# The chunked RWKV-7 recurrence of an encoder kernel: inverse and state in one unrolled body, 32x32 blocks transposed by VectorE, MLP down-products in a pair

## The chip, the cores and the metric

One core of a Trainium2 chip runs the kernel in one launch. The metric is device microseconds. Three runs of the kernel before took 2734.05, 2734.75 and 2739.23 us.

## The reference, cut to what matters

Two layers on a sequence of 1024 rows of 1024 columns. Layer 0 mixes with a gated convolution (512 columns) and RWKV-7 (8 heads of 64), layer 1 with windowed attention; each is followed by an MLP. All is float32. The change is in the RWKV-7 scan and in both MLPs:

```python
    def step(state, inp):
        r_t, w_t, k_t, v_t, a_t, b_t = inp
        sa = jnp.einsum("bhvk,bhk->bhv", state, a_t)
        state = (state * w_t[:, :, None, :] + sa[..., None] * b_t[:, :, None, :]
                 + v_t[..., None] * k_t[:, :, None, :])
        return state, jnp.einsum("bhvk,bhk->bhv", state, r_t)
...
def squared_relu_mlp(h, w_up, w_down):
    return jnp.square(jax.nn.relu(h @ w_up)) @ w_down
```

## The kernel before, in words

The residual, its norm and all weights of the running product lie in SBUF with model columns on the 128 partitions. Dense products are done in three passes of fp32r halves (`product`, L245): high times high, low times high, high times low. Stages follow each other: input projection, recurrence, output projection, MLP 0, QKV, attention, output, MLP 1.

**The recurrence** goes over NT = 8 chunks of 128 rows. For each chunk there are four pieces of work.
- prep (L634 to L768) makes a, b, k and r with their decays from the projected rows: lora products on TensorE (L665, L671), adds, a scan, and products on VectorE, sigmoids, exponentials and a root on ScalarE, squares summed and spread per head (L620, L626), the bonus (L686).
- the solve needs the inverse of a unit triangular 128x128 matrix for each of 8 heads. `chunk_pe` (L888) transposes a, b, k, v to token-major (L895), forms the masked products p1 and p2 (L913; VectorE masks them into mt_rb and nt_rk, L1050), starts the inverse tri_inv_t from pairs of rows (GpSimd L1106, L1109), transposes it (L923), and doubles the solved block in LEVELS = 6 levels. In levels 0 to 3 each is y = x_level times tri_inv (L947), copied by ScalarE (L1025), and then two products dt and dtt (L958, L961), which VectorE adds to the inverse and to its transpose (L1083, L1085); all are 128x128 per head, with masks x_level from GpSimd (L1113). Levels 4 and 5 work on 32x32 and 64x64 blocks (L847, L859, L862; L872, L884).
- the state part: w_t (L971), z (L975), u (L986), the output `o` (L981, L989, L997) and the new state (L965, L992, L1094, L1096).
- out (L771 to L831): group norm per head, gate and bonus of the chunk's output.

The order is written by hand. `recurrence` (L1122) does prep of chunk 0, then for each chunk the whole solve and state, with the pieces of prep of the next chunk and of out of the one before put between the levels, then out of the last chunk, with the splits of the output projection's operand beside it. Chunk 0 and chunk 7 stand alone, chunks 1 to 6 are a hardware loop of three turns with two chunks each. Each engine has its own queue in this order, and each step adds to a semaphore (`Track`, L558) for which the others wait. The state of a chunk ends before the next chunk's inverse starts.

**An MLP group** (L288, 8 groups in each of two MLPs) is four up-products, whose results go through VectorE (L447), ScalarE (square, then the high half, L423, L425) and VectorE (the low half mlp_lo, L450), and eight down-products of four k-steps each, which VectorE adds to the residual (L455). The first down-product waits in k-step k for mlp_lo k.

## Time and profile before

| | us |
|---|---|
| median of the runs | 2734.75 |
| the profiled execution | 2739.59 |
| its span, first to last instruction | 2737.8 |
| TensorE busy / VectorE / ScalarE / GpSimd | 2587.3 / 1136.0 / 696.1 / 320.1 |
| mean granted TensorE clock, share of 2.4 GHz | 0.979 |

Matmuls are pipelined: the busy time of TensorE is the union of records that overlap, and each record's duration has latency in it that the next one hides. The issue time of a group is its length less the latency of one record.

### The profile page before, as it was taken

The page shows a single profiled execution, that of the slowest core. Times are in us where ns is not written, and L with a number is a line of the kernel's source. Part 1 is how long each engine was busy: PE and PEld are TensorE (multiplying, and loading weights), DVE is VectorE, ACT ScalarE, POOL GpSimd, SP SyncE. Part 2 cuts the span into 40 slices and gives each one's busy share as a digit, 9 for nine tenths or more (in the row PEclk, how much of TensorE's full clock was granted, in tenths as well). Part 3 has the DMA queues.
Part 4 walks back from the last instruction along what each step waited for, and adds up shares of the span by engine and source line. Part 5 has one row for each costly group of instructions (what it writes and reads, how often), then busy time and mean ns, then how long its engine had stood idle before and what let it go on. Part 6 is the DMA issues. An engine that isn't in the chain of part 4 may idle for free.

```text
span 2737.8 us, 34644 instructions
## 1 busy us (share of the span) xinstructions
PE 2587.3 (95%) x13906; PEld 2140.4 (78%) x13906; DVE 1136.0 (41%) x1331; ACT 696.1 (25%) x1053; POOL 320.1 (12%) x242
## 2 busy tenths in 40 slices
PE   6999899898989999999999999977999999999998
PEld 5888688787887788888888878744778888888887
DVE  3344466666643333323333343277333332333332
ACT  4010134433321211211122122265231121112212
POOL 0000033332323200000000040043310000000000
PEclk8999999999989999999999999999999999999999
DMA  3221000000011111111111111100111111111112
GB/s 109 79 60 52 15 1 1 2 1 2 13 35 52 41 47 47 54 46 46 47 52 46 46 41 54 31 1 0 42 44 47 47 54 46 46 46 53 46 46 77
DMA packets 166311, 110.54 MB, mean 40 GB/s; under 512 B 3582, under 2 KB 163668, under 8 KB 166228
## 3 DMA queue, kind: packets, MB, share of 16 engines
q1 hardware_dynamic: 163756, 100.39, 12.3%
q0 software_dynamic: 2416, 8.91, 1.0%
q8 instruction: 66, 1.08, 0.2%
q14 instruction: 17, 0.14, 0.0%
q10 hardware_dynamic: 56, 0.01, 0.0%
HBM read 102.49 MB, written 6.29 MB: 40 GB/s over the span
## 4 chain that ended last, share of the span: by engine, by line
PE 83%; DVE 9%; ACT 4%; issue 3%; DVEq 0%; DMA 0%; POOL 0%; SPq 0%; ACTq 0%; POOLq 0%
PE ps L261 70%; PE ps L958 1%; PE ps L1368 1%; PE ps L961 1%; PE ps L947 1%; DVE probs L1396 1%; DVE softmax_stats L1401 1%; PE ps L913 1%; DVE mlp_lo L450 1%; DVE stage L447 1%; PE ps L975 1%; ACT stage L423 1%; PE ps L895 1%; ACT mlp_hi L425 1%; DVE x_level L1059 1%
## 5 line engine op out<-in xcount | busy, mean ns | idle before, releaser
L261 PE MATMUL ps<-h_hi,w_hi 128*128 128x512 f32 x1856 | 579.2, 393 | 23.3 <-DVE h_lo L1706 10.1
L261 PE MATMUL ps<-h_lo,w_hi 128*128 128x512 f32 x1856 | 575.6, 391 | 0.0
L261 PE MATMUL ps<-h_hi,w_lo 128*128 128x512 f32 x1856 | 574.3, 391 | 0.0
L222 ACT CAST w_hi<-w_raw 128x1024 fp32r<-128x1024 f32 x180 | 189.3, 1052 | 966.1 <-PE ps L261 966.1
L261 PEld LDWEIGHTS ps<-h_hi,w_hi 128*128 128x128 f32 x1856 | 347.8, 189 | 98.4 <-issue 14.8
L261 PEld LDWEIGHTS ps<-h_lo,w_hi 128*128 128x128 f32 x1856 | 350.8, 189 | 74.0
L261 PEld LDWEIGHTS ps<-h_hi,w_lo 128*128 128x128 f32 x1856 | 350.6, 189 | 73.8
L261 PE MATMUL ps<-mlp_hi,w_hi 128*128 128x512 f32 x1024 | 317.7, 391 | 10.7 <-DVE mlp_lo L450 10.7
L261 PE MATMUL ps<-mlp_lo,w_hi 128*128 128x512 f32 x1024 | 315.5, 389 | 0.0
L261 PE MATMUL ps<-mlp_hi,w_lo 128*128 128x512 f32 x1024 | 315.4, 389 | 0.0
L455 DVE TENSOR_TENSOR residual<-residual,ps 128x1024 f32<-128x1024 f32 x128 | 156.2, 1220 | 355.8 <-PE ps L261 355.8
L226 DVE TENSOR_TENSOR w_lo<-w_raw,w_hi 128x1024 fp32r<-128x1024 f32 x180 | 219.4, 1219 | 98.8 <-ACT w_hi L222 98.7
L261 PEld LDWEIGHTS ps<-mlp_hi,w_hi 128*128 128x128 f32 x1024 | 190.4, 188 | 55.7 <-DVE mlp_lo L450 17.5
L447 DVE SCALAR_TENSOR_TENSOR stage<-ps,rms_inverse 128x1024 f32<-128x1024 f32 x64 | 78.4, 1225 | 365.3 <-PE ps L261 365.3
L261 PEld LDWEIGHTS ps<-mlp_hi,w_lo 128*128 128x128 f32 x1024 | 192.2, 188 | 40.3
L261 PEld LDWEIGHTS ps<-mlp_lo,w_hi 128*128 128x128 f32 x1024 | 192.2, 188 | 40.2
L423 ACT ACTIVATE stage<-stage 128x1024 f32<-128x1024 f32 x64 | 67.8, 1060 | 535.9 <-DVE stage L447 535.9
L334 POOL TENSOR_TENSOR stage<-residual 128x1024 f32<-128x1024 f32 x21 | 54.4, 2592 | 794.8 <-DVE residual L455 678.9
L450 DVE TENSOR_TENSOR mlp_lo<-stage,mlp_hi 128x1024 fp32r<-128x1024 f32 x64 | 78.5, 1226 | 141.2 <-ACT mlp_hi L425 141.2
L403 DVE TENSOR_TENSOR stage<-ps,rms_inverse 128x1024 f32<-128x1024 f32 x31 | 38.0, 1225 | 130.0 <-PE ps L261 127.8
L958 PE MATMUL ps<-y_level,tri_inv_t 128*128 128x128 f32 x512 | 71.2, 283 | 9.0 <-ACT y_level L1025 9.0
L1025 ACT COPY y_level<-ps 128x512 f32<-128x512 f32 (+2 forms) x96 | 47.7, 511 | 114.5 <-PE ps L947 47.1
(249 smaller groups left out, 2451.3 us busy)
## 6 DMA issues: line engine op xcount, KB each, us to landing
w_raw<-in_mlp_up SPq DMA_DIRECT2D x64, 512.0 KB, 4.0
w_raw<-in_mlp_down SPq DMA_DIRECT2D x64, 512.0 KB, 3.4
w_raw<-in_w_in_ab SPq DMA_DIRECT2D x26, 512.0 KB, 3.9
w_raw<-in_w_qkv SPq DMA_DIRECT2D x10, 512.0 KB, 3.9
x_in_tile<-in_x POOLq DMA_DIRECT2D x8, 512.0 KB, 4.2
w_raw<-in_w_out_ab SPq DMA_DIRECT2D x8, 512.0 KB, 4.1
w_raw<-in_w_o SPq DMA_DIRECT2D x8, 512.0 KB, 3.9
out<-out_chunk SPq DMA_DIRECT2D x8, 512.0 KB, 3.2
```

Of the source, the lines that this page charges most:

```text
L222: nc.scalar.copy(WH[:, slot], WR[:, slot]).then_inc(w_hi, 1)
L226: nc.vector.tensor_tensor(WL[:, slot], WR[:, slot], WH[:, slot].bitcast(F32), ALU.subtract).then_inc(w_lo, 1)
L261: m = nc.tensor.matmul(acc(a_slot, half), ww, xx[:, k, half * HALF:(half + 1) * HALF], start=first, stop=last)
L334: TT((ST1 if k else ST2)[:, 0:S], X[:, k], X[:, k], ALU.mult).then_inc(sq_pool, 1)
L403: nc.vector.tensor_tensor(dst, acc2(slot), RI[:, :], ALU.mult).then_inc(acc_free[slot], 1)
L423: nc.scalar.activation(ST1[:, 0:S], ST0[:, 0:S], ACT.Square).then_inc(relu_sq, 1)
L425: nc.scalar.copy(ACh[:, j], ST1[:, 0:S]).then_inc(act_hi, 1)
L447: nc.vector.scalar_tensor_tensor(ST0[:, 0:S], acc2(j % 2), 0.0, RI[:, :], ALU.max, ALU.mult)\
L450: nc.vector.tensor_tensor(ACl[:, j], ST1[:, 0:S], ACh[:, j].bitcast(F32), ALU.subtract).then_inc(act_lo, 1)
L455: nc.vector.tensor_tensor(X[:, m], X[:, m], acc2(m % 2), ALU.add)\
L958: m = MM(bank(3 * b + 1)[:, j], TIT[:, 4 * b + j], YL[:, 4 * b + j], start=True, stop=True)
L1025: T.done(nc.scalar.copy(dst, src), f"y{k}_{b}")
```

## The change

The recurrence is rewritten as one body per engine, called with n = -1 to 8 in plain Python, so all of it is straight-line code. Body n does the inverse of chunk n, the state and the output of chunk n-1, and prep of chunk n+1; the steps of the three are interleaved. In body 7 there is no prep, in body 8 only state and output.

The inverse is done first for the four diagonal 32x32 blocks of each head alone: `diag` forms them straight from a and b (weights of 64 rows and 32 columns), VectorE copies them out (mtc), builds the start and transposes it with its 32x32 transpose. In levels 0 to 3 y and dt are 8 heads by 4 blocks of 32x32; dt adds in PSUM to the inverse that an identity product put there, and VectorE alone copies the sum (i) and transposes it (tt) out of PSUM. There is no dtt. GpSimd makes all three further masks in one instruction, and copies the four blocks into the full transposed inverse. Levels 4 and 5 join the blocks as before. The row products p1, p2 take two products of 128 columns in place of one of 256, as a, b, k lie in ABK and r in RDEC; the transposes to tokens come after them. Both lora products read the projected rows directly, on row halves 0 to 63 and 64 to 127, one behind the other, and write two banks. The state is kept scaled for the next chunk (GG), in 64x64 blocks. u accumulates onto the z part in one bank. The read-back of the conv rows is issued by GpSimd after tok3 of chunk 7; before, it was issued after v of chunk 7 had been copied.

The order on TensorE in a full body is: lora products; diag; w_t, z part; y0; u; identity product; n2; dt0; output part 1 (L981, L989 before); y1; output part 2, new state; dt1; y2; p1_0; dt2; mean; y3; p1_1; nt; dt3; p2_0; var; y4; p2_1; dt4, dtt4; vt; tok0, tok1; y5; bonus; tok2, tok3; dtt5; gate; nv. On VectorE: mtc, i, tt, ti, x0; the first three of prep; i0, tt0; u; scan to dx, gg; i1, tt1; four state steps; ka, k2; i2, tt2, m0; max, rcp; d; i3, tt3, m1, n0; rcp; kkn, a_dec; t4, tt4, n1; b0, b_dec; m1 of out; tt5; k_dec, r_dec; m4, yb; bonus. On ScalarE: square; w_t; y0; two sigmoids; y1; g, e1; o; y2; e2, e1x, root; square of out; y3; spread; half (two copies); root of out; y4; spread of out; tok0, tok1; y5; tok2, tok3; nv.

In the MLP the first two down-products are issued as a pair: k-steps 0 to 2 of the first, 0 and 1 of the second, then 3 of the first, 2 and 3 of the second.

The diff, cut to its core:

```diff
+            def first_pair(g, after):
+                t.wait_ge(w_lo, u0 + 8 * g + 4 + 3)
+                t.wait_ge(acc_free[0], a0_ // 2 + 6 * g + 3)
+                for n, (m, k) in enumerate(((0, 0), (0, 1), (0, 2), (1, 0), (1, 1), (0, 3), (1, 2), (1, 3))):
+                    if n < 3 or k == 3:
+                        t.wait_ge(act_lo, 4 * NG * l + 4 * g + 2 + k)
+                    if n == 3:
+                        t.wait_ge(acc_free[1], a0_ // 2 + 6 * g + 3)
+                    if after and (m, k) == (1, 3):
+                        after(t, 0)
+                    w_h = WH[:, 0, k * 256 + P * m:k * 256 + P * m + P]
+                    w_l = WL[:, 0, k * 256 + P * m:k * 256 + P * m + P]
+                    for ww, xx in ((w_h, ACh), (w_h, ACl), (w_l, ACh)):
+                        first, last = k == 0 and ww is w_h and xx is ACh, k == 3 and ww is w_l
+                        for half in range(2):
+                            i = nc.tensor.matmul(acc(m, half), ww, xx[:, k, half * HALF:(half + 1) * HALF],
+                                                 start=first, stop=last)
+                    if k == 3:
+                        i.then_inc(acc_done, 1)
...
+                first_pair(g, after)
+                for m in range(2, 8):
                     product(t, m // 2 % 2, m % 2, a0_ // 2 + 6 * g + 2 + m // 2, u0 + 8 * g + 4 + m // 2,
-                            GF, 256, P * (m % 2), ACh, ACl,
-                            ready=(act_lo, 4 * NG * l + 4 * g + 1) if m == 0 else None,
-                            new_unit=m % 2 == 0,
-                            between={2: lambda m=m: after(t, m - 1)} if after and m else None)
+                            GF, 256, P * (m % 2), ACh, ACl, new_unit=m % 2 == 0,
+                            between={2: lambda m=m: after(t, m - 1)} if after else None)
...
+        inv_pe = Track("inverse_pe", ["diag", "y0", "dt0", "y1", "dt1", "y2", "p1_0", "dt2", "y3", "p1_1", "dt3", "p2_0",
+                                      "y4", "p2_1", "dt4", "dtt4", "tok0", "tok1", "y5", "tok2", "tok3", "dtt5", "nv"])
+        inv_act = Track("inverse_act", ["y0", "y1", "y2", "y3", "half", "y4", "tok0",
+                                        "tok1", "y5", "tok2", "tok3", "nv"])
+        inv_dve = Track("inverse_dve", ["mtc", "i", "tt", "ti", "x0", "i0", "tt0", "i1", "tt1", "i2", "tt2", "m0", "i3", "tt3", "m1", "n0", "t4", "tt4_0",
+                                        "tt4_1", "n1", "tt5"])
+        inv_pool = Track("inverse_pool", ["x"] + [f"full{q}" for q in range(4)])
+        st_pe = Track("state_pe", ["wt", "u", "o", "s"])
+        st_act = Track("state_act", ["wt", "o"])
+        st_dve = Track("state_dve", ["u", "gg", "s1_0", "s1_1", "s2_0", "s2_1"])
...
+        B_T, B_Y, B_M, B_PREP, B_OUT = 0, 1, (2, 3), 6, 7
...
+        def body_pe(t, n):
...
+            def diag_products(bank_n, left, right, start):
+                for h in range(8):
+                    for q in range(4):
+                        m = MM(block_bank(bank_n, 32)[quarter(q), h], left[quarter(q), h], right[quarter(q), h],
+                               start=start == "each" or start == "first" and h == 0, stop=True, skip_group_check=True)
+                return m
+            def level_y(k):
+                if k:
+                    inv_dve.wait(t, n, f"i{k - 1}")
+                    inv_pool.wait(t, n, "x")
+                else:
+                    inv_dve.wait(t, n, "x0")
+                inv_pe.done(diag_products(B_Y, XLC[:, k], TIC, "each"), f"y{k}")
+            def level_dt(k):
+                inv_act.wait(t, n, f"y{k}")
+                if k:
+                    inv_dve.wait(t, n, f"tt{k - 1}")
+                inv_pe.done(diag_products(B_T, TTC, YLC, "none"), f"dt{k}")
...
+            def row_products(q, b):
...
+                for j in two:
+                    for par in two:
+                        rows = half_rows(par)
+                        out_ = PS[:, B_M[par], 2 * P * j:2 * P * j + 2 * P].rearrange("p (a m) -> p a m", m=P)
+                        left = ABK[rows, s, 1 + q, 2 * b + j]
+                        MM(out_[:, 0], left, ABK[rows, s, 0, 2 * b + j], start=True, stop=True)
+                        m = MM(out_[:, 1], left, RDEC[rows, s, 2 * b + j], start=True, stop=True)
+                inv_pe.done(m, f"p{q + 1}_{b}")
...
+            if inv:
+                level_dt(1)
+                level_y(2)
+                row_products(0, 0)
+                level_dt(2)
+            if state:
+                st_act.wait(t, c, "o")
+                out_pe.done(MM(bank(B_OUT), blk, part(c, 4), start=True, stop=True), "mean")
+            if inv:
...
+            if inv:
+                inv_dve.wait(t, n, "m1")
+                for b in two:
+                    top, low = quarter(2 * b), quarter(2 * b + 1)
+                    for h in range(8):
+                        m = MM(block_bank(B_Y, 32)[low, h], MTRB[top, h, 0, low], TIC[top, h], start=True, stop=True)
+                inv_pe.done(m, "y4")
+                row_products(1, 1)
...
+            def block_transpose(k):
+                inv_pe.wait(dve, n, f"dt{k}")
+                W.done(nc.vector.tensor_copy(TIC[:, :], block_bank(B_T, 32)[:, 0:8]), f"i{k}")
+                W.done(nc.vector.transpose(TTC[:, :], block_bank(B_T, 32)[:, 0:8]), f"tt{k}")
...
+                W.wait(dve, n, "mtc")
+                W.done(TT(TTC[:, :], MTC[:, :], diag_const(C_M0), ALU.mult), "i")
+                W.wait(dve, n, "i")
+                W.done(TT(TTC[:, :], TTC[:, :], diag_const(C_I32), ALU.add), "tt")
+                W.wait(dve, n, "tt")
+                W.done(nc.vector.transpose(TIC[:, :], TTC[:, :]), "ti")
+                W.done(TT(XLC[:, 0], MTC[:, :], diag_const(C_MX), ALU.mult), "x0")
+            if prep:
...
-                    for j in range(4):
-                        m = MM(bank(3 * b + 1)[:, j], TIT[:, 4 * b + j], YL[:, 4 * b + j], start=True, stop=True)
-                    T.done(m, f"dt{k}_{b}")
-                    for j in range(4):
-                        m = MM(bank(3 * b + 2)[:, j], YL[:, 4 * b + j], TIT[:, 4 * b + j], start=True, stop=True)
-                    T.done(m, f"dtt{k}_{b}")
-
...
-            recurrence(t, chunk_pe, prep_pe_step, out_pe_step)
+            for n in range(-1, NT + 1):
+                body_pe(t, n)
```

## Rows read from the trace of the kernel before

**Rows 1.** Page, part 1: busy time, share of the span, instructions of each engine.

```profile
PE 2587.3 (95%) x13906; PEld 2140.4 (78%) x13906; DVE 1136.0 (41%) x1331; ACT 696.1 (25%) x1053; POOL 320.1 (12%) x242
```

**Rows 2.** Table of stretches of the recurrence: busy time, granted clock (PEclk), DMA.

```profile
324.00:344.90 20.90, 8.28 (x32) 5.70 (x30) 15.56 (x23) 7.10 (x11) 4.93 (x5) 0.64 0.00 0
344.90:398.90 54.00, 52.23 (x518) 48.05 (x518) 35.52 (x51) 19.46 (x33) 20.52 (x18) 0.95 0.00 1
398.90:754.60 355.70, 321.37 (x3243) 290.84 (x3241) 228.40 (x337) 141.23 (x234) 115.61 (x102) 1.00 0.02 6
754.60:827.80 73.20, 62.30 (x533) 57.12 (x532) 33.80 (x47) 19.66 (x34) 14.99 (x12) 0.79 0.10 30
```

**Rows 3.** Timeline, TensorE, starts of chunks 3 and 4 (start, length, instruction).

```profile
518.45 0.65 PE L895 MATMUL ps<-constants,a_r_dec 128*128 128x128 f32 x4 [2.77 <-issue]
...
576.87 0.66 PE L895 MATMUL ps<-constants,a_r_dec 128*128 128x128 f32 x4
```

**Rows 4.** Timeline, TensorE, 500 to 523 us: groups of the same records.

```profile
500.51 1.02 PE L686 MATMUL ps<-prep_t,constants 128*128 128x512 f32 x2
501.46 0.59 PE L859 MATMUL ps<-y_level,tri_inv_t 32*32 32x32 f32 x13
...
501.87 0.21 PE L862 MATMUL ps<-tri_inv_t,y_level 32*32 32x32 f32 x1
...
508.51 2.00 PE L975 MATMUL ps<-nv_part,tri_inv_t 128*128 128x64 f32 x16
...
510.44 1.09 PE L981 MATMUL ps<-nt_rk,token_major 128*64 128x128 f32 x16
...
521.38 2.00 PE L913 MATMUL ps<-a_r_dec,b_k_dec 64*128 64x256 f32 x16
```

**Rows 5.** Waits of the weight loads, 330 to 830 us: total, times, longest.

```profile
PEld ps L671 <- issue: 2.3, 7, 0.3
...
PEld ps L975 <- issue: 1.5, 8, 0.3
```

**Rows 6.** Waits of TensorE, 324 to 828 us: total, times, longest.

```profile
PE ps L958 <- ACT y_level L1025: 9.0, 6, 1.6
...
PE ps L847 <- DVE tri_inv L1083: 5.8, 8, 0.9
PE ps L895 <- issue: 5.6, 2, 2.8
```

**Rows 7.** Groups by line and shape, VectorE and ScalarE, 320 to 800 us: busy, mean.

```profile
L1085 DVE TENSOR_TENSOR tri_inv_t<-tri_inv_t,ps 128x512 f32<-128x512 f32 x64 | 43.7, 683 | 6.0 <-PE ps L961 6.0
...
L1050 DVE TENSOR_TENSOR mt_rb<-ps,constants 128x1024 f32<-128x1024 f32 x16 | 18.8, 1220 | 5.6 <-PE ps L913 5.6
...
L1074 DVE COPY tri_inv<-ps 32x256 f32<-32x256 f32 x16 | 6.8, 424 | 20.0 <-PE ps L859 19.8
...
L1025 ACT COPY y_level<-ps 128x512 f32<-128x512 f32 x64 | 36.0, 584 | 47.1 <-PE ps L947 47.1
```

**Rows 8.** Table of stretches of chunk 7, as rows 2.

```profile
794.00:797.00 3.00, 3.00 (x83) 2.84 (x81) 1.93 (x5) 0.23 (x1) 0.00 (x0) 1.00 0.00 0
...
800.00:807.00 7.00, 7.00 (x42) 6.33 (x42) 0.00 (x0) 0.91 (x2) 0.00 (x0) 0.50 0.00 0
```

**Rows 9.** Timeline, TensorE, 807 to 815 us, the end of chunk 7.

```profile
806.57 1.98 PE L981 MATMUL ps<-nt_rk,token_major 128*64 128x128 f32 x16
...
811.52 1.06 PE L992 MATMUL ps<-u_part,token_major 128*128 128x128 f32 x8
812.51 1.09 PE L997 MATMUL ps<-mt_rb,u_part 128*64 128x128 f32 x16
```

**Rows 10.** The MLP: timeline of one group, then the waits of the whole span.

```profile
1060.74 0.73 PE L261 MATMUL ps<-mlp_hi,w_hi 128*128 128x512 f32 x2 [0.67 <-DVE mlp_lo L450]
...
1067.87 1.22 DVE L455 TENSOR_TENSOR residual<-residual,ps 128x1024 f32<-128x1024 f32 x1 [4.22 <-PE ps L261]
...
PE ps L261 <- DVE mlp_lo L450: 10.7, 16, 0.7
```

More of the change, by code:

```diff
@@ L594, in hybrid_trunk @@
         out_pool = Track("out_pool", ["m2"])
-        state_zero = sem("state_zero")
-        def part(c, first):
-            return RKV[:, first:first + 4, bass.ds(c * P, P)]
-        def heads(ap, b):
-            return ap[:, 4 * b:4 * b + 4]
-        HEAD = ("before the masks", "between the masks", "after the masks")
-        LEVEL = tuple((k, b) for k in range(LEVELS) for b in two)
-        PLACES = HEAD + LEVEL[0:2] + (0,) + LEVEL[2:4] + (1, "root") + sum(
-            ((k,) + LEVEL[2 * k:2 * k + 2] if k != 4 else LEVEL[8:10] + (4,) for k in (2, 3, 4, 5)), ()) + ("end",)
@@ new lines, in body_pe @@
+            if state:
+                out_dve.wait(t, c, "m1")
+                for p in range(4):
+                    m = MM(bank(B_OUT)[:, p], LOR[:, 2, p * P:(p + 1) * P], GL[:, c * P:c * P + P],
+                           start=True, stop=True)
+                out_pe.done(m, "gate")
+            if inv:
+                inv_dve.wait(t, n, "n1")
+                inv_act.wait(t, n, "tok3")
+                for h in range(8):
+                    m = MM(PS[:, B_M[0], RH * h:RH * h + RH], NTRK[:, h, 0], TOK[:, 3, RH * h:RH * h + RH],
+                           start=True, stop=True)
+                inv_pe.done(m, "nv")
@@ L701, in prep_act_step @@
                 prep_act.done(A(T2[:, :], T3[:, :], ACT.Exp, scale=-KAPPA), "e1")
+            if state:
+                st_pe.wait(act, c, "o")
+                waited(act, "act")
+                st_act.done(nc.scalar.copy(part(c, 4), bank(B_OUT)), "o")
+            if inv:
+                level_y(2)
+            if prep:
                 prep_act.wait(act, e, "e1")
                 prep_act.done(A(T3[:, :], T3[:, :], ACT.Exp, scale=KAPPA), "e2")
-            if place == 1:
                 prep_act.done(A(T4[:, :], T4[:, :], ACT.Exp, scale=-KAPPA), "e1x")
+            if prep:
@@ new lines, in body_act @@
+            if state:
+                out_pe.wait(act, c, "var")
+                out_act.done(A(VR[:, :], PS[:, B_OUT, 0:2 * NP_], ACT.Sqrt, bias=VT[:, 91:92], scale=1.0 / RH), "sd")
+            if inv:
+                evict("y4", YLC[:, :], block_bank(B_Y, 32)[:, 0:8])
+            if n == NT:
+                mixed_act(act, 2)
+            if state:
+                out_dve.wait(act, c, "rcp")
+                dst, src = by_head(SQO[:, :], VR[:, :])
+                out_act.done(nc.scalar.copy(dst, src), "spread")
@@ L748, in prep_dve_step @@
                 V.done(nc.vector.reciprocal(NR[:, :], NR[:, :]), "rcp")
-            if place == (2, 0):
-                V.done(TT(AR[:, s, :, 1], part(e, 0), T2[:, :], ALU.mult), "r_dec")
-            if place == (3, 0):
+            if state:
+                out_pe.wait(dve, c, "mean")
+                out_dve.done(STT(part(c, 4), bank(B_OUT), -1.0 / RH, part(c, 4), ALU.mult, ALU.add), "d")
+            if n == NT:
+                mixed_dve(dve, 0)
+                mixed_dve(dve, 1)
+            if inv:
+                block_transpose(3)
+                masked_products(0, 1, "m1")
+                masked_products(1, 0, "n0")
@@ new lines, in body_dve @@
+            if state:
+                out_pe.wait(dve, c, "vt")
+                out_dve.done(TT(part(c, 4), part(c, 4), bank(B_OUT), ALU.mult), "m1")
+            if inv:
+                inv_pe.wait(dve, n, "dtt5")
+                W.done(nc.vector.tensor_copy(TIT[0:RH, :, RH:P], block_bank(B_T, RH)[0:RH]), "tt5")
+            if prep:
+                V.done(TT(ABK[:, e % 2, 2], T0[:, :], T3[:, :], ALU.mult), "k_dec")
+                if state:
+                    st_pe.wait(dve, c, "o")
+                V.done(TT(RDEC[:, e % 2], part(e, 0), T2[:, :], ALU.mult), "r_dec")
@@ new lines, in body_dve @@
+            if state:
+                out_pool.wait(dve, c, "m2")
+                prep_pool.wait(dve, c, "lb")
+                out_dve.done(TT(part(c, 4), part(c, 4), BON[:, c % 2], ALU.add), "m4")
+                out_pe.wait(dve, c, "gate")
+                out_dve.wait(dve, c, "m4")
+                out_dve.done(TT(part(c, 0), part(c, 4), bank(B_OUT), ALU.mult), "yb")
+            if prep:
+                prep_pe.wait(dve, e, "bon")
+                V.done(TT(BON[:, e % 2], bank(B_PREP), part(e, 8), ALU.mult), "bon")
@@ L1710, in _ @@
             dve.wait_ge(late_in, 16 * N_LATE)
[L1711 to L1712 removed]
+            for n in range(-1, NT + 1):
+                body_dve(dve, n)
             for k in range(4, KD):
```

831 lines of the change are left out of this document (350 added, 481 removed).

## The prediction

> **What bounds the kernel now.** I read the page's engine lines first: TensorE is busy for 95% of the span, VectorE for 41%, ScalarE for 25% [rows 1]. So time is won only where TensorE waits or does less. Then I cut out the stage that is rewritten, with a table of stretches [rows 2]: from the end of the input projection (324.0 us) to the first product of the output projection (827.8 us) it takes 503.8 us: 20.9 us of preparing chunk 0, 54.0 us for chunk 0, 355.7 us for chunks 1 to 6 (59.3 each), 73.2 us for chunk 7 and its tail. In chunks 1 to 6 TensorE is busy for 321.4 of 355.7 us at the full clock.
>
> The timeline gives a chunk inside the loop: 518.45 to 576.87, 58.4 us [rows 3]. I split it with issue times. A record (each fp32 product of two operands is two, a transpose one) with 128 weight columns costs 2.00 us for 16, some 0.112 us each behind its 0.28 us of latency [rows 4]. Levels 0 to 3 are 48 such records each, 21.5 us together; all records of a chunk come to 50.6 us by the same kind of sum. When the tile of the array changes shape, the next weight load starts 0.2 to 0.3 us late: "issue" of 1.5 us in 8 before L975, 2.3 us in 7 before L671 [rows 5]. A chunk has 15 such changes, 3 us at 0.2. The waits on other engines, led by 9.0 us for y_level and 5.8 us for tri_inv over the stage [rows 6], leave about 5 us per chunk. 50.6 + 3 + 5 = 58.6 against 58.4 measured, so the method is fit for the new order. Each turn of the loop adds 2.8 us of "issue" (5.6 us in two) [rows 6], which is why the mean is 59.3.
>
> **The change, part by part, in one steady chunk.**
> (1) The inverse works on diagonal 32x32 blocks: y and dt of levels 0 to 3, the identity product and `diag` are 10 groups of 64 records, in place of four levels of 48 wide records, the four transposed-inverse products and the two transposes t0. What does one cost? Records that stay in one 32x32 tile follow each other every 0.033 us (13 in 0.59 us with 0.19 us of latency); but L862 starts at 501.87 while L859 is still issuing, so tiles overlap [rows 4]. L913 shows how far: 16 records of 256 columns take 2.00 us, though 512 columns cost 0.43 us (two records in 1.02 us, latency off), so one after another they'd take 3.4: its two row halves run side by side [rows 4]. The new loop goes round four tiles. The bounds are 64 x 0.033 = 2.1 us in series and 0.5 us at four abreast; I take 0.77 us (0.012 per record), since both rows show overlap. Ten groups: 7.7 us.
> (2) All other records of the new body, by the same row prices (the row products are split in two but at half the width, so still 0.86 us each; both lora products at once on the two row halves, 0.86 instead of 1.8): 25.0 us. TensorE issues 32.7 us.
> (3) The body changes tile shape 31 times instead of 15, since every small group stands between wide ones: 31 x 0.2 = 6.2 us.
> (4) Waits. VectorE costs 0.68 us for 128x512, 1.22 for 128x1024, 0.42 for 256 columns; ScalarE 0.58 for 512 [rows 7]. No row has VectorE's 32x32 transpose. Bounds: 0.42 us as the copy of the same 256 columns, 0.84 at half that speed; I take the first, as it is the same read of PSUM (the second adds at most 2 us). Walking the queues in their written order, TensorE waits for w_t's copy (queued on ScalarE behind the square of the next chunk) 0.8 us; y2 for i1, with nothing between dt1 and y2, 0.8; nt for the spread, which ScalarE does behind square and y3, 2.0; the row product p2_0 for m1, which VectorE queues behind i3 and tt3 and so behind dt3, 2.2; tok0 for n1, queued behind dtt4, 1.6; the next lora products for bonus, 1.2. Sum 8.6. VectorE has 32 us of work and GpSimd 8: neither is the bound, only their order counts. ScalarE loses two table loads; it had room.
> Sum at the full clock: 32.7 + 6.2 + 8.6 = 47.5, say 48 us, 11 less than 59.3.
> (5) The clock. From 794 to 797 us TensorE is busy 3.00 of 3.00 us, yet with 32- and 64-row tiles, and at 797.2 its granted clock goes from 2.4 to 1.2 GHz and stays there past 807 under products of all 128 rows [rows 8]; L981 then takes 1.98 us instead of 1.09 [rows 4, 9]. Before, small tiles lie together for about 5 us per chunk. Afterwards they're spread over all of it, and from nt's wait to tok0 (some 14 us) there are only small or half-height groups, a 2-column product and three waits. I expect the clock to fall there in each chunk and to be back around the transposes to tokens, bonus and gate, which use all rows. Walking p2_0 to dtt5 with doubled issue, 11 us of TensorE work, moves dtt5 by 9.8 us; in some chunks it lasts longer. I take +11; the bounds are 0 and +28 (all of the chunk, 32.7 us more less what the waits absorb). A chunk: 59 us.
> (6) Ends. Preparing chunk 0 is shorter by 3.4 us (17.5 instead of 20.9): both lora products are out before VectorE needs them, and the first product waits for b_dec, not for k_dec and the bonus. Chunk 0 has no state and no output beside it, so it is a bare chain at half clock, 51 us against 54. The body of chunk 7 with the state of 6: 51 us. The last body is a chain from w_t to the output's last product: w_t to `o` 12.5 us at half clock, then the same tail as before, 812.5 to 827.8 less `o` itself [rows 2, 9], 14.5 us: 27. The conv rows' read-back is now issued behind tok3 of chunk 7; it has about 14 us before ScalarE wants it and takes 8, so it costs nothing; if late, the tail grows by the difference. GpSimd's m2 stands behind its issue, under 1 us, long before m1. SP's weight loads wait for p2_1, which comes earlier in its body.
> Stage: 17.5 + 51 + 6 x 59 + 51 + 27 = 500.5, 3 us less than 503.8.
> (7) MLP pairs. In each of the 16 groups TensorE waits 0.67 us for the last mlp_lo (10.7 us in 16) [rows 10]. The new order puts 12 products (2.7 us at 0.226) of the second output block in front of it; the wait is gone, and the first block's sum is ready 2.7 us later, where VectorE idled 4 us ahead of the next sum [rows 10]. -10.7 us, which nothing else claims; at worst -5.
> **Sum:** -3.3 - 10.7 = -14 us. The profiled execution took 2739.6 us (span 2737.8), so 2725.6; the median of the runs is 4.8 us lower, hence 2734.75 - 14 = 2721.
>
> **A rule against the change.** The Trainium skill (TensorEngine Tiling (Array Packing), Gotcha 1: PSUM Pressure) says that different row tiles can't access one PSUM bank at the same time. All four tiles of a new group write one bank, in different partitions; L913's two halves write two banks, so the trace doesn't decide. The same page (Key Properties) says that a changed tiling mode drains the engine; with the 0.2 us of [rows 5] the trace agrees.
>
> **Rivals.**
> A, the clock holds. For it: in chunks 1 to 6 it stayed at 1.00 on average [rows 2], through 5 us of small tiles each. Against it: 797 us, and the waits of (4). Then a chunk is 48 us and chunk 7 46: 2721 - 66 - 5 = 2650. Chance 0.18.
> B, slower: the clock falls and isn't granted again within the body, since few stretches use all rows for long. It decides from +14 us of stretch per chunk on; at +22 a chunk is 70 us: 2721 + 66 + 5 = 2792. For it: after 797 it took till some 811, mostly under full-height products, to come back [rows 9]. Chance 0.22.
> C, the groups go one tile after another, by a bank or a queue: 10 x (2.1 - 0.8) = 13 us per chunk, of which waits hide 3: 6 x 10 + 10 = +70, 2791. For it: most pairs of L859 and L862 don't overlap. Against it: those share row groups, and L913. Chance 0.15.
> D, nothing comes of the rewrite because VectorE's in-order queue delays more than I found; only the pairs count: 2724, within my forecast.
> Forecast (with D): 0.45, its own range 2690 to 2752 (a chunk between 54 and 64).
>
> **How the numbers follow.** About 0.2% (5.5 us) is what a measurement can tell from no change. Of the forecast's 0.45, 0.30 lies below 2729, 0.07 within, 0.08 above. With A, faster 0.48; with B and C, slower 0.45. The range reaches from just below A's 2650 (2648) to just past B's and C's (2800).
>
> **What would show it.** Right: TensorE records of one small group at about 0.012 us; a granted clock between 0.7 and 0.85 over the stage, with the fall after nt; waits before nt, p2_0 and tok0 of about 2 us; no wait on mlp_lo. A granted clock near 1.00 means A, below 0.65 B; 2 us per small group C. Wrong altogether if VectorE is busy for most of a chunk, or if "issue" grows in the unrolled code.

## The result, and the profile after

The changed kernel takes 2690.28 us (median of 4 runs, 2688.44 to 2696.72) beside 2736.42 us for the kernel before on the same chip (4 runs, 2734.05 to 2739.23): a ratio of 0.9835, interval 0.9815 to 0.9855, 46 us less. The forecast was 2721, 14 us less, so the gain is more than three times the forecast. The sign was right. The time lies well inside the wide range (2648 to 2800), but only 0.3 us inside the forecast's own (2690 to 2752).

The profiled execution took 2696.72 us, span 2694.7 (before: 2739.59 and 2737.8, so the two profiles differ by 43 us). Page of the changed kernel, the lines that answer to [rows 1], then the granted clock in 40 slices:

```profile
PE 2525.9 (94%) x17650; PEld 2077.5 (77%) x17650; DVE 1062.8 (39%) x1286; ACT 643.9 (24%) x985; POOL 230.3 (9%) x180
...
PEclk7999957777869999999999999899999999999999
```

In the slices of the recurrence, the sixth to the twelfth, the clock is at 5 to 8. The table of stretches shows where the time went (us, busy time and count of TensorE, weight loads, VectorE, ScalarE, GpSimd, then granted clock, DMA share, GB/s); its stretches answer to [rows 2], and the last is all that follows:

```profile
324.30:346.40 22.10, 8.14 (x51) 5.36 (x49) 15.16 (x22) 7.07 (x11) 5.21 (x6) 0.64 0.00 0
346.40:396.40 50.00, 38.56 (x882) 33.73 (x880) 23.59 (x40) 14.30 (x25) 6.96 (x8) 0.53 0.01 2
396.40:724.10 327.70, 278.67 (x6059) 241.18 (x6057) 173.05 (x305) 97.47 (x179) 47.02 (x53) 0.76 0.01 2
724.10:800.30 76.20, 60.90 (x1086) 53.65 (x1085) 28.47 (x44) 16.52 (x29) 7.44 (x9) 0.69 0.16 50
800.30:2694.70 1894.40, 1838.76 (x8267) 1494.51 (x8266) 686.83 (x758) 448.76 (x675) 155.93 (x85) 0.99 0.15 45
```

The first stretch is the preparation of chunk 0, the second chunk 0, the third chunks 1 to 6, the fourth chunk 7 and the last body. The stage takes 476.0 us in place of 503.8 (-27.8; forecast -3.3), and what follows 1894.4 in place of 1910.0 (-15.6; forecast -10.7). Chunks 1 to 6 are 54.6 us each (forecast 59, before 59.3) at a granted clock of 0.76: (1 - 0.76) x 2 x 327.7 / 6 = 26 us of each are at 1.2 GHz. Around chunk 3 (508.4 to 562.1 us), stretches cut where the clock changed:

```profile
481.00:511.00 30.00, 28.83 (x283) 25.19 (x281) 12.42 (x20) 4.67 (x9) 3.25 (x3) 0.50 0.00 1
511.00:535.00 24.00, 19.22 (x720) 16.45 (x718) 15.54 (x32) 11.27 (x20) 3.19 (x3) 0.99 0.02 4
535.00:555.00 20.00, 17.67 (x154) 15.09 (x155) 8.14 (x12) 3.39 (x8) 2.61 (x5) 0.50 0.01 2
```

Timeline of chunk 3 in the changed kernel, TensorE (start, length, instruction, in brackets the idle time before it); it answers to [rows 3, 4]. L659 issues the small groups, 64 records on 32x32 tiles:

```profile
514.73 1.16 PE L750 MATMUL ps<-state_in,w_t 128*128 128x128 f32 x8 [0.88 <-ACT w_t L894]
515.82 0.75 PE L659 MATMUL ps<-constants,diag_inv_t 32*32 32x32 f32 x64
516.50 1.05 PE L758 MATMUL ps<-constants,prep_t 128*128 128x2 f32 x8
517.49 0.74 PE L659 MATMUL ps<-diag_y,diag_inv_t 32*32 32x32 f32 x63
...
524.65 0.65 PE L659 MATMUL ps<-diag_inv,diag_x 32*32 32x32 f32 x53 [0.52 <-DVE diag_inv L977]
525.94 0.31 PE L659 MATMUL ps<-diag_inv,diag_x 32*32 32x32 f32 x11 [0.64 <-issue]
...
532.84 0.66 PE L805 MATMUL ps<-constants,prep_t 128*128 128x128 f32 x4 [1.46 <-ACT prep_t L934]
533.42 0.75 PE L659 MATMUL ps<-diag_y,diag_inv_t 32*32 32x32 f32 x64
536.16 0.80 PE L690 MATMUL ps<-a_b_k_dec 64*128 64x128 f32 x4 [1.99 <-DVE mt_rb L970]
...
548.55 1.97 PE L701 MATMUL ps<-constants,a_b_k_dec 128*128 128x128 f32 x8 [1.17 <-DVE nt_rk L970]
...
560.99 0.37 PE L710 MATMUL ps<-decay_aaa_in,lora_w 64*128 64x128 f32 x1 [1.15 <-DVE bonus L1099]
```

The waits stand where the prediction put them: w_t 0.88 (0.8 forecast), y2 on i1 0.52 (0.8), nt 1.46 (2.0), p2_0 on m1 1.99 (2.2), tok0 on n1 1.17 (1.6), lora on bonus 1.15 (1.2). All idle time of TensorE in this chunk comes to 8.3 us (8.6 forecast), of which 0.9 is "issue" and not a wait for another engine.

Three things follow from these lines, all at the full clock. First, the price of a small record: 64 records take 0.75 us, 53 take 0.65 and 11 take 0.31, so 0.008 us each; in reorder, below, 56 take 0.69 and 8 take 0.26, 0.009 us each. That is the lower bound of step (1), four tiles abreast (64 x 0.033 / 4 = 0.53 us), where 0.012 was taken. Second, a group's successor starts 0.68 us behind it (515.82 to 516.50), so that some 0.1 to 0.15 us are left for the change out of the small shape. Third, the change into it lies in the group ahead. The 8 records of 2 columns stand ahead of a small group now, which starts 0.99 us behind them (516.50 to 517.49). In the kernel before, the same records stood ahead of a group of their own shape, which started 0.80 us behind them:

```profile
533.08 0.95 PE L620 MATMUL ps<-constants,prep_t 128*128 128x2 f32 x8
533.88 1.14 PE L958 MATMUL ps<-y_level,tri_inv_t 128*128 128x128 f32 x8
```

So the change in costs 0.19 us, as the prediction had it. From the start of chunk 0 to the end of the stage, TensorE's waits (total, times, longest), which answer to [rows 6]:

```profile
PE ps L690 <- DVE mt_rb L970: 17.5, 13, 2.0
PE ps L701 <- DVE nt_rk L970: 10.4, 8, 2.2
PE ps L659 <- DVE diag_x L995: 8.3, 6, 3.7
PE ps L805 <- ACT prep_t L934: 8.3, 6, 1.5
```

One was not foreseen, on diag_x. It is 3.7 us in chunk 0; in chunk 3 other products cover it. The timeline of VectorE and of GpSimd at the start of chunk 3 shows where it comes from, as in every chunk:

```profile
509.78 0.42 DVE L990 TENSOR_TENSOR diag_inv_t<-diag_mt,constants 128x256 f32<-128x256 f32 x1
510.24 1.92 DVE L992 TENSOR_TENSOR diag_inv_t<-diag_inv_t,constants 128x256 f32<-128x256 f32 x1
```

```profile
509.83 2.05 POOL L1108 TENSOR_TENSOR diag_x<-diag_mt,constants 128x768 f32<-128x768 f32 x1 [3.65 <-DVE diag_mt L987]
```

L992 is the same kind and size as L990, which began before GpSimd's instruction and took 0.42 us. L992 began beside it, took 1.92 us, and ended 0.3 us after it.

### The profile page after: what moved, and what is told of

Same layout as the page of the kernel before. It is cut to its first block, busy times and chain, and to the rows that moved or that the text cites. A ratio compares the mean times of both kernels' runs of the same rounds, so it can differ in the third digit from the quotient of the medians.

```text
span 2694.7 us, 40848 instructions
## 1 busy us (share of the span) xinstructions
PE 2525.9 (94%) x17650; PEld 2077.5 (77%) x17650; DVE 1062.8 (39%) x1286; ACT 643.9 (24%) x985; POOL 230.3 (9%) x180
## 4 chain that ended last, share of the span: by engine, by line
PE 88%; DVE 8%; ACT 2%; issue 1%; POOL 0%; DMA 0%; SPq 0%; DVEq 0%; ACTq 0%
PE ps L265 67%; PE ps L310 6%; PE ps L659 2%; PE ps L690 1%; PE ps L701 1%; PE ps L1358 1%; DVE probs L1386 1%; DVE softmax_stats L1391 1%; PE ps L1327 1%; DVE mt_rb L970 1%; PE ps L691 1%; PE ps L1172 1%; DVE diag_inv_t L992 1%; PE ps L847 1%; PE ps L852 1%
## 5 line engine op out<-in xcount | busy, mean ns | idle before, releaser
L265 PE MATMUL ps<-mlp_hi,w_lo 128*128 128x512 f32 x768 | 236.6, 389 | 0.0
L265 PEld LDWEIGHTS ps<-mlp_hi,w_lo 128*128 128x128 f32 x768 | 144.2, 188 | 29.9
L265 PEld LDWEIGHTS ps<-mlp_lo,w_hi 128*128 128x128 f32 x768 | 144.2, 188 | 29.9
L265 PEld LDWEIGHTS ps<-mlp_hi,w_hi 128*128 128x128 f32 x768 | 143.8, 188 | 29.4
```

The lines of the kernel that those rows point to most:

```text
L265: m = nc.tensor.matmul(acc(a_slot, half), ww, xx[:, k, half * HALF:(half + 1) * HALF], start=first, stop=last)
```

## The experiments

Times are medians; "base" is the changed kernel, 2690.28 us. Where chunks are told apart, a chunk runs from the first product of `diag` to the next one's. The kernel before took 2733.0 to 2740.7 us (medians) beside these runs, single ones 2728.67 to 2760.03. The runs lie on several chips, so a difference of medians between two changed kernels is uncertain by some us; each ratio is to the kernel before on the same chip.

**pairs_alone**: the kernel before with the changed kernel's `mlp_pe`.

```diff
-                for m in range(8):
+                first_pair(g, after)
+                for m in range(2, 8):
```

> The kernel before, with the MLP's pair order alone; the recurrence is the old one. Theory (step 7 of the prediction): the wait on the last mlp_lo, 10.7 us in 16 groups, goes and nothing else changes: 2736.4 - 10.7 = 2725.7 us. Rival: the whole 15.6 us by which the stages behind the recurrence became shorter in the changed kernel (1910.0 to 1894.4 us) comes from the pairs, because the clock or the units behind the first product gain too: 2720.8 us. Second rival: the 4.9 us above 10.7 belong to the hand-over from the recurrence, and then they are missing here.

2719.15 us (10 runs, 2711.87 to 2731.94), ratio 0.994 (0.9914 to 0.9967): 15 us less, between 9 and 24. What follows the recurrence takes 2711.5 - 819.6 = 1891.9 us, not 1910.0. The period of an MLP group, between two VectorE instructions at the same place of it, in the kernel before and in this one:

```profile
1023.38 1.23 DVE L447 SCALAR_TENSOR_TENSOR stage<-ps,rms_inverse 128x1024 f32<-128x1024 f32 x1 [8.53 <-PE ps L261]
...
1111.39 1.23 DVE L447 SCALAR_TENSOR_TENSOR stage<-ps,rms_inverse 128x1024 f32<-128x1024 f32 x1 [8.52 <-PE ps L261]
```

```profile
1012.87 1.23 DVE L466 SCALAR_TENSOR_TENSOR stage<-ps,rms_inverse 128x1024 f32<-128x1024 f32 x1 [8.52 <-PE ps L261]
...
1099.91 1.23 DVE L466 SCALAR_TENSOR_TENSOR stage<-ps,rms_inverse 128x1024 f32<-128x1024 f32 x1 [8.52 <-PE ps L261]
```

88.01 and 87.04 us: 0.97 us a group, 15.5 us in 16, where [rows 10] gave 0.67. In the kernel before, the starts of the products ahead of, at and behind the wait show the same loss:

```profile
1059.45 0.61 PE L261 MATMUL ps<-mlp_hi,w_lo 128*128 128x512 f32 x2
1060.74 0.73 PE L261 MATMUL ps<-mlp_hi,w_hi 128*128 128x512 f32 x2 [0.67 <-DVE mlp_lo L450]
1061.31 0.62 PE L261 MATMUL ps<-mlp_lo,w_hi 128*128 128x512 f32 x2
```

The pairs are 1.29 and 0.57 us apart, where all others are 0.45 to 0.46: 0.95 us lost. The idle time of the product (0.67) is too short, that of the weight load (1.1) a little too long:

```profile
PEld ps L261 <- DVE mlp_lo L450: 17.5, 16, 1.1
```

The product's idle time begins at the end of the last product's record, 0.61 us behind its start, though the next could have started 0.45 us behind it. So the first rival's number holds, but not its reason: the 15.5 us are the wait itself, read too short, and no gain of the clock or of other units is needed. The second rival falls, since nothing is missing here; the 2.6 us by which this stretch is shorter than the pairs explain are not accounted for. This execution also had an old recurrence of 495 us (324.3 to 819.6), against 503.8 in the profile of before; from 754.6 us on, the granted clock was 0.93 here and 0.79 there. Some 8 of the 27.8 us that the two profiles differ by in the stage may be such a difference between executions. By the medians the pairs give 15 us and the rewrite 31 (with the interval of the pairs, 22 to 37).

**groups_tile_by_tile**

```diff
-                for h in range(8):
-                    for q in range(4):
+                for q in range(4):
+                    for h in range(8):
```

> The changed kernel, with the eight products of one 32x32 tile issued one after another and then the next tile's, in place of going round the four tiles. Theory: it is the rotation that lets the four tiles overlap, so a group of 64 records goes from 0.75 us to the 2.1 us of 64 x 0.033; nine groups in each of eight chunks (diag keeps its order) give +1.3 x 72 = 97 us at most, some 70 us after what waits absorb: about 2760 us. Rival (C of the prediction in another form): records of one bank or one queue never overlap, the 0.75 us come from short records alone, and the order changes nothing: 2690 us.

2862.61 us (2 runs), 172 us more than base. Timeline of TensorE, a small group at the full and one at the low clock:

```profile
422.29 1.91 PE L659 MATMUL ps<-constants,diag_inv_t 32*32 32x32 f32 x64
...
431.32 3.06 PE L659 MATMUL ps<-diag_inv,diag_x 32*32 32x32 f32 x64
```

In base a group takes 0.75 and, in chunk 0 at the low clock, 1.08 us. So the order around the tiles is what lets them overlap, all in one bank (each tile in its own 32 partitions), and rival C falls; the rule it leaned on (the Trainium skill, TensorEngine Tiling (Array Packing), Gotcha 1: PSUM Pressure) doesn't bind here, and the measurement decides. Had the groups gone in series, its 2791 us would have been far too low: it left out that the low clock lengthens them too. The expected 2760 was too low by 103 us for the same reason: it priced the groups and not the clock. Chunks 1 to 6 are 75 to 79 us at a clock of 0.57 to 0.62.

**warm**

```diff
+            def warm(k):
+                for i in range(k):
+                    MM(bank(4)[:, i % 4], ident, ident, start=True, stop=True)
...
+                    warm(4)
                     prep_dve.wait(t, n, "bon")
...
+                warm(5)
                 prep_act.wait(t, e, "spread")
...
                 level_dt(3)
+                warm(8)
...
+                warm(5)
                 to_tokens(0)
```

> The changed kernel, with 5, 8, 5 and 4 products of 128x128 by 128 columns on constants, into a bank that nobody reads, where TensorE waits for nt, p2_0, tok0 and the next lora products (at the full clock 0.225 us each; they change no output). Theory 1 (the stretch by the clock is as predicted, 11 us a chunk, and the full-clock body is cheaper than the predicted 48 us): the clock stays at 1.00 and a body goes from 54.6 to some 44 us, the kernel to about 2610 us. Theory 2 (the full-clock body is 48 us as predicted and the low clock costs only 6.6 us a chunk): 48 us a body, about 2640 us. Theory 3: the small groups themselves, not the waits, lower the clock, so it falls all the same: the body stays at 54 to 57 us, 2690 to 2710 us.

2644.39 us (4 runs), ratio 0.9645 (0.9601 to 0.9689), 46 less than base. Chunks 1 to 6 take 46.6 to 50.7 us at 0.86 to 0.96; the best of them (table of stretches):

```profile
389.12:435.68 46.56, 42.74 (x1058) 37.24 (x1056) 28.82 (x51) 16.24 (x30) 8.02 (x9) 0.96 0.01 3
```

More work on TensorE, less time: theory 3 falls. The time is theory 2's, but its reason isn't, as the clock wasn't held everywhere; the experiment doesn't separate theories 1 and 2. reorder does: 36.5 us of work at the full clock (below) and 8.3 of idle time are 44.8 us, theory 1's 44.

**m1_first** (the semaphore's list is put in the same order)

```diff
             if inv:
+                masked_products(0, 1, "m1")
                 block_transpose(3)
-                masked_products(0, 1, "m1")
...
-                inv_dve.wait(t, n, "m1")
+                inv_dve.wait(t, n, "i3")
                 for b in two:
```

> The changed kernel with one of the three moved steps alone: on VectorE the mask m1 ahead of i3 and tt3. In the changed kernel p2_0 waits 2.0 us for it in each of eight chunks. Theory 1 (waits alone count, the clock is a thing of its own): 16 us less, 2674 us. Theory 2 (a wait inside the stretch of small products also brings the fall of the clock, so that taking it away gives more than its own length): the share of the stage at the low clock falls clearly too, and the kernel takes less than 2665 us. Theory 3 (what stood behind it is late next: nt, tok0): less than 8 us, 2682 us or more.

2653.85 us (2 runs), 36 us less. The wait on mt_rb falls from 17.5 to 2.6 us, so 15 us of waits were worth 36. The clock rose from 0.53 to 0.64 in chunk 0, and from between 0.70 and 0.80 to between 0.74 and 0.89 in chunks 1 to 6. Theory 2.

**reorder**: the edit of m1_first, and (in `body_dve`, then in `body_act`)

```diff
+                masked_products(1, 1, "n1")
                 inv_pe.wait(dve, n, "dt4")
...
-                masked_products(1, 1, "n1")
...
+            if prep:
+                prep_dve.wait(act, e, "rcp")
+                dst, src = by_head(T6[:, :], NR[:, :])
+                prep_act.done(nc.scalar.copy(dst, src), "spread")
+            if inv:
+                level_y(3)
             if state:
                 out_dve.wait(act, c, "d")
...
-            if inv:
-                level_y(3)
-            if prep:
-                prep_dve.wait(act, e, "rcp")
-                dst, src = by_head(T6[:, :], NR[:, :])
-                prep_act.done(nc.scalar.copy(dst, src), "spread")
```

> The changed kernel, with three steps moved on their in-order queues: on VectorE the mask of p1_1 (m1) ahead of the copies i3 and tt3, and the mask n1 ahead of t4, tt4_0 and tt4_1; on ScalarE the spread ahead of y3, and the output's square behind y3. Theory: the waits of step 4 are queue order and nothing else. In the changed kernel they are 17.5 us for mt_rb, 10.4 us for nt_rk and 15.4 us for the spread over the stage; they go, and 43 us of waits become at least 30 us of time: 2655 us. Rival: what stands behind each wait (dt3's y3, dt4, y5) is late too and takes over, under 12 us come out: 2680 us or more.

2616.8 us (4 runs), ratio 0.9554 (0.9509 to 0.96), 73 less than base. The three waits fell from 36.2 (17.5, 10.4, 8.3) to 2.8 us. The theory's direction holds, but 2655 was too high by 38 us: here too a wait was priced at its length at most. It has a chunk wholly at the full clock:

```profile
384.64:425.95 41.31, 36.43 (x1015) 31.72 (x1013) 29.35 (x51) 16.24 (x30) 8.05 (x10) 1.00 0.01 3
```

Its idle times in the timeline are 0.77, 0.98, 0.22, 0.52, 0.69, 0.43 and 1.15, together 4.8 us (three of them "issue", 1.3). That leaves 36.5 us of issue and shape changes, the same products in the same order as in base.

**transpose_twice**

```diff
+                nc.vector.transpose(SPARE[:, :], block_bank(B_T, 32)[:, 0:8])
                 W.done(nc.vector.transpose(TTC[:, :], block_bank(B_T, 32)[:, 0:8]), f"tt{k}")
```

> The changed kernel, with each of the four block transposes of a chunk's levels on VectorE done once more, into a spare tile, ahead of the real one (it changes no output). It prices the operation that step 4 took at 0.42 us. Theory 1: only the time of the last queue counts, since the transpose stands beside the next level's products: +0.44 us in front of m1 alone, 3.5 us over eight chunks, 2694 us. Theory 2: the levels are a chain through VectorE and each transpose lies on it: 4 x 0.44 x 8 = 14 us, 2704 us.

2695.34 us (2 runs, 2694.37 and 2696.31), 5 more by the medians, though base's runs reach 2696.72; the wait on mt_rb rises from 17.5 to 24.1. It is nearer theory 1 (2694) than theory 2 (2704). The transpose takes 0.44 us (0.42 forecast).

**reorder_x**

```diff
-                inv_dve.wait(pool, n, "mtc")
+                inv_dve.wait(pool, n, "x0")
+                if prep:
+                    prep_dve.wait(pool, e, "kkr")
```

> The reordered kernel with GpSimd's level masks behind VectorE's kkr, and nothing else of combo. Theory: L992 takes 0.42 us in place of 1.92, y0 comes up to 0.8 us earlier in each chunk and 1.5 us earlier in chunk 0: 7 us, with the clock up to 15 us less than reorder, 2602 to 2610 us. Rival: GpSimd's 2 us then lie beside other VectorE instructions and slow those, 2617 us.

2594.43 us (4 runs, 2586.84 to 2604.07), ratio 0.946 (0.9399 to 0.9522), 22 less than reorder, more than the theory had. The wait on diag_x is left in chunk 0 alone (2.2 us).

**reorder_lora** (TensorE's part; VectorE then reads banks 4 and 5)

```diff
-                    prep_dve.wait(t, n, "bon")
-                if c > 0:
-                    out_dve.wait(t, c - 1, "yb")
+                    prep_dve.wait(t, n, "zas")
...
-                    mw = MM(bank(B_PREP)[:, p], LOR[0:RH, 0, p * P:(p + 1) * P], WA[0:RH, e * P:e * P + P],
+                    mw = MM(bank(4)[:, p], LOR[0:RH, 0, p * P:(p + 1) * P], WA[0:RH, e * P:e * P + P],
...
-                    ma = MM(bank(B_OUT)[:, p], LOR[RH:P, 1, p * P:(p + 1) * P], WA[RH:P, e * P:e * P + P],
+                    ma = MM(bank(5)[:, p], LOR[RH:P, 1, p * P:(p + 1) * P], WA[RH:P, e * P:e * P + P],
```

> The reordered kernel with the lora products in two banks of their own, and nothing else of combo. combo brought 35 us, where its two edits were to take away 16 us of waits. Theory (the clock follows the waits): the wait on the bonus, 1.15 us in each of 7 chunks, goes, and the clock's fall with it in some chunks: 12 to 20 us less than reorder, 2597 to 2605 us. Rival: this edit gives its 8 us and no more, 2609 us, and the rest belongs to GpSimd's instruction.

2622.22 us (4 runs, 2617.50 to 2630.65), 5 more than reorder, whose runs reach 2623.14: no gain, a miss for both. The wait on the bonus is gone, but four chunks in a row take 47.8 to 47.9 us at 0.79, each with two stretches of 10 us at the low clock, where reorder's took 41 to 46. Fewer waits do not by themselves mean fewer falls: where the waits that are left lie counts.

**combo**: both edits on top of reorder.

> The reordered kernel (2616.8 us), and two waits more taken away: the next chunk's lora products go into two banks that nobody else uses, so they no longer wait for the bonus and the output that VectorE reads last; and GpSimd's instruction for the level masks starts behind VectorE's kkr, not behind mtc, so that it no longer runs beside L992, which took 1.92 us in place of 0.42. The reordered kernel shows 6.4 us of waits in 6 on the bonus and 9.8 us in 8 on diag_x (3.7 of it in chunk 0). Theory: about 1.1 us a chunk for the first (8 us), and up to 1 us a chunk for the second (8 us): 2600 us, with L992 back at 0.42 us. Rival: the wait on the bonus moves one step on, to diag, which needs tt5 and b_dec, and GpSimd now slows other instructions of VectorE's: 2612 us or more.

2581.55 us (4 runs, 2572.18 to 2598.37), ratio 0.946 (0.9425 to 0.9495): 151 us less than the kernel before beside it, and 109 less than base. Against reorder_x it is 13 us less by the medians and nothing by the ratios, so what the lora edit adds here is not shown. Its VectorE row of L992 (L988 here) is back at 425 ns, and GpSimd's instruction, now beside L997 and L999, which have one operand in PSUM, doesn't slow them (684 and 681 ns):

```profile
L997 DVE TENSOR_TENSOR prep_t<-ps,vectors 128x512 f32<-128x512 f32 x7 | 4.8, 684 | 0.0
L999 DVE TENSOR_TENSOR prep_t<-ps,vectors 128x512 f32<-128x512 f32 x7 | 4.8, 681 | 0.0
...
L988 DVE TENSOR_TENSOR diag_inv_t<-diag_inv_t,constants 128x256 f32<-128x256 f32 x8 | 3.4, 425 | 0.3
```

Stretches of combo, chunks 1 to 4:

```profile
380.48:418.06 37.58, 35.90 (x1014) 31.56 (x1012) 27.89 (x51) 16.24 (x30) 7.50 (x9) 1.00 0.01 3
418.06:461.74 43.68, 41.03 (x1015) 35.58 (x1013) 27.48 (x52) 16.43 (x30) 7.78 (x9) 0.88 0.01 3
461.74:499.97 38.23, 35.88 (x1014) 31.56 (x1013) 27.54 (x52) 16.24 (x30) 7.78 (x9) 1.00 0.02 4
499.97:538.08 38.11, 35.82 (x1014) 31.56 (x1013) 27.55 (x52) 16.25 (x30) 7.78 (x9) 1.00 0.01 3
```

The same work costs 38 us at the full clock and 43.7 with 10 us of it at the low one: 5.5 us for a fall. The small products are those of base, and the clock holds through them; they alone don't bring the fall.

**n1_late** and **n1_late_filled**: combo with the mask n1 behind tt4_1 again, and the same with the wait filled.

```diff
-                masked_products(1, 1, "n1")
                 inv_pe.wait(dve, n, "dt4")
...
+                masked_products(1, 1, "n1")
...
+                warm(8)
                 to_tokens(0)
```

> combo with one wait put back: VectorE's mask n1 again behind t4, tt4_0 and tt4_1, so that the transposes to tokens wait for it, 1.2 to 2.2 us in each of eight chunks (as in the changed kernel). combo is at the full clock in five of its eight chunks, so the price of one wait can be read there. Theory 1 (a wait in the stretch of small products costs its length and brings a fall of the clock, which costs some 5 us per chunk that it hits): 13 us of waits and 10 to 30 us of clock, 2605 to 2625 us, and a fall in chunks that had none. Theory 2 (a wait costs its length): 2590 to 2597 us, the clock as in combo.

> The same kernel, with eight dummy products of 128x128 by 128 columns (1.8 us at the full clock) in that wait. The wait for n1 ends no earlier, so VectorE's queue costs the same; only TensorE works on the whole array meanwhile. Theory 1: the clock is held, and of the time that n1_late loses against combo the clock's part comes back: 2590 to 2600 us. Theory 2: there is nothing to come back, 2590 to 2600 us in both. Rival: the dummies change nothing in the clock, which falls by the small products ahead of the wait: as n1_late, or some us more.

2620.25 us (4 runs, 2600.34 to 2633.31) and 2589.77 us (4 runs, 2589.24 to 2597.68). The wait put back is this row of n1_late:

```profile
PE ps L701 <- DVE nt_rk L966: 11.8, 8, 2.2
```

By the medians 12 us of waits cost 39 us, and filled with products that nobody uses they cost 8. combo ran on another chip; by the ratios (0.9537 for n1_late, 0.9449 filled, 0.946 for combo) the two costs are 21 us and nothing, so the wait cost some 20 to 40 us, and the filled wait's price is within the noise. Both kernels ran on one chip, where the filled one is 30 us faster (24 by the ratios) and its slowest run faster than the other's fastest. Chunk 3 of n1_late, then of n1_late_filled:

```profile
477.18:524.94 47.76, 44.65 (x1014) 38.88 (x1012) 27.78 (x51) 16.54 (x30) 7.78 (x9) 0.79 0.01 3
```

```profile
466.35:506.42 40.07, 37.65 (x1031) 33.33 (x1029) 27.28 (x52) 16.14 (x30) 7.77 (x9) 1.00 0.01 4
```

VectorE's queue is the same in both. Only what TensorE does in the wait differs, so the 30 us are the clock's: chunks 1 to 6 are at 0.72 to 0.85 in n1_late and at 0.85 to 1.00 with the wait filled. Theory 1. The fill was made of products on the whole array, so it is not shown that small products in the same place would have held it too.

**combo_ends**: dummies in combo's waits of the preparation, chunk 0 and the last output.

```diff
+                warm(2, n == 0)
                 inv_act.wait(t, n, f"y{k}")
...
+                warm(30, n == -1)
                 prep_act.wait(t, e, "spread")
```

> combo with dummy products of 128x128 by 128 columns (on constants, into a bank not in use) in the waits of the two ends: 52 in the preparation of chunk 0, 2 before each level product and 8 before the first in chunk 0, 28 in the output of the last chunk. There combo is at the low clock: 328 to 368 us, and from 659 to 678 us. Theory: the clock is held by work on the whole array in the waits, also where the waits themselves stay: chunk 0 goes from 36.2 to 32 or 33 us, the preparation loses 1 us and the tail with the first output products 4 us; 2573 us. Rival: the chain of small products in chunk 0 lowers the clock all the same, and the dummies then cost twice their time and stand in front of what they were to cover: 2585 us or more.

2586.4 us (4 runs, 2583.47 to 2589.05), 5 more than combo, within the spread of combo's runs. That is the rival's time (2585 or more), but not for its reason. The ends did as the theory says in direction: chunk 0 is at 1.00 in place of 0.72 and takes 34.8 us in place of 36.2, and starts 2.8 us earlier. But chunks 1, 3 and 5 now have a fall (42.5 to 43.5 us at 0.88) where in combo one of the six (chunk 2) had it in full. Nothing is won on the whole.

## Why the prediction was right or wrong

**The sum of a chunk.** Point by point, in us, with the measured values from above:

| term of the prediction | forecast | measured |
|---|---|---|
| (1), (2), (3) issue and shape changes | 38.9 | 36.5 (in reorder's chunk at the full clock) |
| (4) waits | 8.6 | 8.3 |
| (5) stretch by the clock | 11 | 9.8, the rest to 54.6 |
| a chunk | 59 (the sum, 58.5, was rounded up) | 54.6 |

The step that failed is this sum: each chunk came out 4.4 us shorter than forecast. The term mis-sized most is (1), the small group. It was taken at 0.012 us a record, 0.77 us, between bounds of 0.5 and 2.1; the records take 0.008 to 0.009, some 0.55 us, close to full overlap of the four tiles. Ten groups are thus 2.2 us less, nearly all of the 2.4 in the first line. The changes of tile shape (3) were about right: 0.19 us in and 0.10 to 0.15 out, where 0.2 was taken for each. The stretch by the clock gave 1.2 us more, the waits 0.3, the rounding 0.5. The forecast was a small difference of two large numbers: six times 4.4 is 26 us, on a forecast of -3.3 for the stage. All four errors went the same way. That the time still fell inside the forecast's own range, by 0.3 us, is luck.

**The ends (6).** Preparation took 22.1 us, not 17.5. In the body's order the next chunk's lora products, which wait 2.0 us for the bonus and take 2.0 at the low clock, stand ahead of `diag`; the walk passed over them. Chunk 0 took 50.0 (51), chunk 7 52.3 (51), the last body 23.9 (27). Together the ends are 1.8 us longer than forecast. "Issue" did not grow in the unrolled code: 3.6 us of TensorE's idle time, 5.6 before.

**The MLP (7).** Right in its mechanism (no wait on mlp_lo is left), wrong in its size: 15.5 us, not 10.7, because the wait was read as the product's idle time (0.67 us) and not from the spacing of the products (0.95).

**The clock.** That it falls in each chunk, with the waits before and around the row products, was right. In chunk 3 it fell at 535 us, in the wait for m1 behind nt, and came back at 555, in the transposes to tokens. Over the stage it was 0.72 (0.76 in chunks 1 to 6), where 0.7 to 0.85 was expected. Two things were missed. The fall of chunk 2 lasted 30 us, across the lora products and `diag` of the next chunk. And (4) and (5) are no separate terms. This did not spoil the forecast, as both sizes were nearly right, but it would spoil the price of any change to a wait: m1_first shows 2.4 us for 1 (36 for 15), and n1_late 1.8 to 3.3 (21 to 39 for 12). A (the clock holds) did not come by itself, but with other queue orders it does: base without three waits has a chunk of 41.3 us at 1.00. B came in one chunk of six: the fall of chunk 2 went on into the next body, and in the others the clock came back within the body, so the kernel as a whole is not slower. C fell with groups_tile_by_tile, which shows both that the rotation carries the change and what it would cost without it. D fell as well: the rewrite gave 31 of the 46 us.

**Open.** Which chunk has a fall is not settled. reorder_lora and combo_ends have fewer waits, or filled ones, and more falls than their neighbours; runs of one and the same kernel differ by 26 us (combo) or 33 (n1_late). With it, how much of the stage's 27.8 us is the kernel's and how much the two profiles' is known only as the difference of the medians.

## What to carry to other kernels

Where TensorE alternates small tiles and waits, look at the granted clock first and price each wait with what it does to the clock. Here, moving one VectorE instruction past its neighbours was worth more than twice the wait that the profile showed, and a wait that could not be moved was filled with products into a free bank, which gave most of its price back (though the same at the two ends, in combo_ends, gave nothing on the whole). Walk the in-order queues for every consumer on TensorE's path, and put what the next matrix product reads ahead of copies needed later. Read what a wait of TensorE costs from the spacing of the products' starts, or at the weight load, not from the product's idle time alone. Let small products go round the tiles.

## What the runs showed of the hardware

- 64 records on four 32x32 tiles take 0.75 us going round the tiles, 1.91 us tile by tile (1.08 and 3.06 at the low clock), into one bank in both orders.
- A change from 128x128 to 32x32 tiles costs 0.19 us (8 records of 2 columns: 0.80 us to a successor of their own shape, 0.99 to a small group).
- The low clock doesn't double a small group (0.75 to 1.08 us), but doubles wide ones (L701, 8 records: 1.04 us in reorder, 1.97 in base).
- 10 us at the low clock cost a chunk of 38 us another 5.5 (combo), and idle TensorE time of 1.2 to 2.2 us a chunk cost 21 to 39 us in eight chunks. The same waits with whole-array products in them cost 8 us or nothing.
- A VectorE instruction with both operands in SBUF, begun beside a GpSimd instruction of 2.05 us, took 1.92 us in place of 0.42. Those with one operand in PSUM, beside the same instruction in combo, were not slowed (0.68).
- VectorE's transpose of 32x32 blocks reads PSUM at the speed of a copy: 0.44 us for 128x256, the copy 0.42.
